# One-hot tiles of the first expert index made on ScalarE by Square and Relu, in 4 of the first 16 batches and in all from the 17th on

## What is computed

```python
q = (hb @ w_q).reshape(C, PEER_HEADS, 2, PEER_DK_HALF)
s = jnp.einsum('thpd,hpnd->thpn', q, sub_keys).astype(jnp.float32)
sv, si = lax.top_k(s, PEER_TOPK)
cand = sv[:, :, 0, :, None] + sv[:, :, 1, None, :]
cidx = si[:, :, 0, :, None] * PEER_NKEYS + si[:, :, 1, None, :]
...
fv, fpos = lax.top_k(cand, PEER_TOPK)
eidx = jnp.take_along_axis(cidx, fpos, axis=-1).reshape(C, PEER_HEADS * PEER_TOPK)
g = jax.nn.softmax(fv, axis=-1).reshape(C, PEER_HEADS * PEER_TOPK)
a = jax.nn.gelu(jnp.einsum('ted,td->te', u_tab[eidx], hb), approximate=False)
return jnp.einsum('te,ted->td', (g * a).astype(hb.dtype), v_tab[eidx])
```

## Time and profile before

| | |
|---|---|
| median of 3 runs | 2018.72 us (2017.43 to 2019.43) |
| the profiled execution | 2019.02 us, span 2017.2 us |
| TensorE matmuls | 1965.7 us busy, 97% |
| VectorE | 1407.0 us, 70% |
| ScalarE | 478.5 us, 24% |
| GpSimd | 919.2 us, 46% |
| DMA | 527.06 MB, 261 GB/s over the span |

### The profile page before, as it was taken

How to read it: one execution, slowest core, us unless ns; L and a number is a source line. 1 busy time by engine, 2 the same in 40 slices (tenths; PEclk the granted TensorE clock), 3 DMA queues, 4 the chain that set the end, 5 groups by cost and what they waited for, 6 DMA issues and landing times.

```text
span 2017.2 us, 27236 instructions
## 1 busy us (share of the span) xinstructions
PE 1965.7 (97%) x10016; PEld 1446.1 (72%) x10016; DVE 1407.0 (70%) x3048; ACT 478.5 (24%) x1005; POOL 919.2 (46%) x683
## 2 busy tenths in 40 slices
PE   9999999999999999999999999999999999999997
PEld 7888875888868875788886666666666666666563
DVE  3742025333374567649999999999999999987767
ACT  4122233133563326621230010100101010010100
POOL 5444432427443753424424555554545544443333
PEclk9999999999999999999999999999999999999999
DMA  6555652515202411134379999999999999999998
GB/s 237 189 189 180 148 144 94 187 64 178 86 9 58 125 35 53 43 125 134 129 285 348 422 422 422 421 422 422 415 422 414 416 419 417 407 421 421 419 422 288
DMA packets 92914, 527.06 MB, mean 261 GB/s; under 512 B 10080, under 2 KB 14608, under 8 KB 43280
## 3 DMA queue, kind: packets, MB, share of 16 engines
q0 software_dynamic: 37728, 270.55, 33.1%
q1 hardware_dynamic: 49680, 246.95, 33.0%
q10 hardware_dynamic: 5408, 8.34, 2.0%
HBM read 518.46 MB, written 7.34 MB: 261 GB/s over the span
## 4 chain that ended last, share of the span: by engine, by line
DMA 28%; DVE 20%; PE 15%; POOL 5%; issue 3%; ACT 1%; DVEq 0%; POOLq 0%; ACTq 0%
DMA work<-in_peer_uv,consts 16%; DMA ring<-in_peer_uv,consts 12%; PE ps L854 9%; DVE tables L2144 3%; POOL work L2790 3%; DVE work L2119 2%; POOL ring L2790 2%; DVE ring L2119 2%; DVE hT L2144 1%; DVE ring L2101 1%; PE ps L1138 1%; PE ps L883 1%; DVE tmp L2178 1%; DVE work L1902 1%; DVE work L1895 1%
## 5 line engine op out<-in xcount | busy, mean ns | idle before, releaser
L1271 PE MATMUL ps<-work,tmp 128*128 128x512 f32 x1008 | 447.5, 597 | 21.0 <-DVE tmp L2178 20.9
L1246 PE MATMUL ps<-hT,work 128*128 128x256 f32 x1984 | 450.2, 381 | 0.0
L2697 POOL TENSOR_TENSOR w_lo<-ring,w_hi 128x1024 fp32r<-128x1024 f32 (+2 forms) x116 | 275.0, 2377 | 334.9 <-ACT w_hi L2249 334.9
L1246 PEld LDWEIGHTS ps<-hT,work 128*128 128x128 f32 x1984 | 373.0, 190 | 75.2 <-issue 29.7
L1271 PEld LDWEIGHTS ps<-work,tmp 128*128 128x128 f32 x1008 | 189.3, 190 | 246.0 <-issue 213.9
L2790 POOL DMA_INDIRECT ring<-in_peer_uv,consts x128 | 237.7, 1857 | 264.8 <-DVE tables L2144 234.9
L2790 POOL DMA_INDIRECT work<-in_peer_uv,consts x128 | 226.3, 1768 | 258.1 <-DVE tables L2144 210.3
L2249 ACT ACTIVATE w_hi<-ring 128x1024 fp32r<-128x1024 f32 (+2 forms) x116 | 120.4, 1041 | 360.1 <-PE ps L854 335.3
L2119 DVE CUSTOM_DVE_ANT_0 ring<-ring,tables 128x1024 f32<-128x1024 f32 x128 | 155.5, 1221 | 52.3 <-DMA ring<-in_peer_uv,consts 50.1
L854 PE MATMUL ps<-w_hi,x_hi 128*128 128x512 f32 (+2 forms) x480 | 184.1, 384 | 1.1 <-DVE tmp L1667 1.1
L2119 DVE CUSTOM_DVE_ANT_0 work<-work,tables 128x1024 f32<-128x1024 f32 x128 | 155.2, 1221 | 42.5 <-DMA work<-in_peer_uv,consts 41.8
(11 more groups left out here) (380 smaller groups left out, 3108.8 us busy)
## 6 DMA issues: line engine op xcount, KB each, us to landing
work<-in_peer_v SPq DMA_DIRECT2D x64, 1024.0 KB
work<-in_u_steps SPq DMA_DIRECT2D x62, 1024.0 KB
ring<-in_a_w_in SPq DMA_DIRECT2D x48, 512.0 KB, 4.1
ring<-in_ada_w SPq DMA_DIRECT2D x48, 512.0 KB, 4.9
ring<-in_peer_w_q SPq DMA_DIRECT2D x32, 512.0 KB, 3.5
ring<-in_a_w_out SPq DMA_DIRECT2D x16, 512.0 KB, 4.1
ring<-in_b_w_in SPq DMA_DIRECT2D x16, 512.0 KB, 4.3
ring<-in_c_in SPq DMA_DIRECT2D x12, 512.0 KB, 3.7
```

Of the source, the lines that this page charges most:

```text
L1246: mm = pe.matmul(ps[:, 4 + s, j * DT:(j + 1) * DT], u[:, s, j, k, :], hT[:, k, GATHERED * P:T], start=(k == 0), stop=(k == KD - 1))
L1271: mm = pe.matmul(ps[:, 2 * t + half, :], tmp[:, s, j * DT + t * P:j * DT + (t + 1) * P], v_ring[:, s, j, half * BANK:(half + 1) * BANK], s ...
L2697: pool.tensor_tensor(w_lo[q % NPIECE][:, 0:n], ring[:, at:at + n], w_hi[q % NPIECE][:, 0:n], ALU.subtract).then_inc(w_split, 1)
```

## The change

ScalarE makes the one-hot of the first index for batches 3, 5, 7 and 11 of region 0 (`ACT_HOT`) and for all batches from 17 on. For each of the 16 tokens it computes (i - x)^2 over the 128 values x, the token's index i being the bias, a column of a new f32 copy of the indices (`i_cols`), and then over the whole tile Relu(1 - square), which is 1 where x is i and 0 elsewhere. In region 0 these four tiles have buffers of their own, in the expert buffers 1, 2 and 5, and the work is cut in halves: half of a tile a turn of the loop, eight squares ahead of the loop. The gathers into those buffers get waits for the spreads that read them: slot 1 for spread 5, slot 2 for spread 7, slot 5 for spread 11. In the steps ScalarE makes batch n+17 in step n, ahead of its copy of the gates of batch n+16.

The late pieces of head 0 stand after batches 0 to 3 instead of 1 to 4. `LATE_AT` is new: four products go ahead of the first spread, one product only follows spreads 4, 6 and 10, and the last late scores follow spread 3 instead of spread 5.

```diff
-LATE_AT = (0, 4, 10, 16, 22, 28, 32, 35, 38, 41, 44, 47, 50, 53, 56, 56, 56)
+LATE_AT = (4, 10, 18, 24, 30, 31, 34, 35, 38, 41, 44, 45, 48, 51, 54, 56, 56)
+LAST_SCORES = 3
+ACT_HOT = (3, 5, 7, 11)
...
+        i_cols = consts[:, NKEYS + 2 * GATHERED * SLOTS:NKEYS + 2 * GATHERED * SLOTS + DT]
+        act_hot = [twins(v) for v in (experts[1][:, 0:D], experts[1][:, D:2 * D], experts[2][:, 0:D], experts[5][:, 0:D])]
...
# TensorE
+            late_products(0, LATE_AT[0])
+            for m in range(RSTEPS):
+                if m in ACT_HOT:
+                    pe.wait_ge(hot_act, ACT_HOT.index(m) + 1)
+                    spread_gates(m, m % 2, act_hot[ACT_HOT.index(m)])
+                else:
+                    spread_gates(m, m % 2, hot_i[m % 2])
+                if m == LAST_SCORES:
+                    key_scores("pqL", "peer_l", 2 * PEER_H - 1, 2 * PEER_H - 1)
+                late_products(LATE_AT[m], LATE_AT[m + 1])
...
-                            spread_gates(n + RSTEPS, s)
+                            pe.wait_ge(hot_act, n + 4)
+                            spread_gates(n + RSTEPS, s, hot_i[s])
...
# VectorE
                 one_hot_j(0, m)
-                one_hot_i(m)
+                if m not in ACT_HOT:
+                    one_hot_i(m)
                 weighted_j(m)
-                if 1 <= m <= 4:
-                    late_piece(0, 3 + m)
+                if m < 4:
+                    late_piece(0, 4 + m)
...
-                    one_hot_i(n + RSTEPS)
+                    if n == 0:
+                        one_hot_i(n + RSTEPS)
...
# ScalarE
+            def square_i(m, buf, tokens=range(BATCH)):
+
+                for t in tokens:
+                    token = m % RSTEPS * BATCH + t
+                    act.activation(buf[:, t // TWIN, :, t % TWIN], iota[:], ACT.Square, scale=-1.0,
+                                   bias=i_cols[:, token:token + 1]).then_inc(squared, 1)
+                squares[0] += len(tokens)
+
+            def hot_from_squares(buf):
+
+                act.wait_ge(squared, squares[0])
+                act.activation(buf, buf, ACT.Relu, scale=-1.0, bias=astat[:, 0, 0:1]).then_inc(hot_act, 1)
+
             act.sem_inc(spread_kept, 2)
+            for i in range(3):
+                drained(act, "pairs", i)
+            act.wait_ge(one_made, 1)
+            act.activation(i_cols, iT, ACT.Copy).then_inc(i_kept, 1)
+            act.wait_ge(i_kept, 1)
+            first, second = range(0, BATCH // 2), range(BATCH // 2, BATCH)
+            square_i(ACT_HOT[0], act_hot[0], first)
             for m in range(RSTEPS):
...
+                hot, half = divmod(m + 1, 2)
+                if hot < len(ACT_HOT):
+                    if hot == 3 and half == 0:
+                        full(act, "pqL", 2 * PEER_H - 1)
+                    square_i(ACT_HOT[hot], act_hot[hot], (first, second)[half])
+                    if half:
+                        hot_from_squares(act_hot[hot])
...
             for n in range(STEPS):
                 if 1 <= n < STEPS - RSTEPS:
                     gelu(n + 1)
+                if n + 1 + RSTEPS < STEPS:
+                    act.wait_ge(spread_summed, n + 1 + RSTEPS + 1)
+                    square_i(n + 1 + RSTEPS, hot_i[(n + 1) % 2])
+                    hot_from_squares(hot_i[(n + 1) % 2])
                 if n + RSTEPS < STEPS:
                     act.wait_ge(dense_coef, n + 1)
                     keep_gates(n // RSTEPS + 1, n + RSTEPS)
...
# GpSimd
+            pool.memset(astat[:, 0, 0:1], 1.0).then_inc(one_made, 1)
...
+                    for last_hot, at in ((1, 1), (2, 2), (3, 5)):
+                        if slot == at:
+                            pool.wait_ge(spread_summed, ACT_HOT[last_hot] + 3)
```

More of the change, by code:

```diff
@@ L647, in network @@
         spread_summed = sem("spread_summed")
+        one_made = sem("one_made")
+        i_kept = sem("i_kept")
+        squared = sem("squared")
+        hot_act = sem("hot_act")
         last_sum = sem("last_sum")
@@ L1229, in _, with spread_gates @@
             key_scores("pqL", "peer_l", LATE_FIRST - 1, LATE_FIRST - 1)
-            def spread_gates(m, s):
+            def spread_gates(m, s, hot):
                 pe.wait_ge(hot_ready, m + 1)
@@ L1236, in spread_gates @@
                     for part in range(PARTS):
-                        mm = pe.matmul(ps[:, 6 + s, t * RKEYS:(t + 1) * RKEYS], hot_i[s][:, t // TWIN, :, t % TWIN],
+                        mm = pe.matmul(ps[:, 6 + s, t * RKEYS:(t + 1) * RKEYS], hot[:, t // TWIN, :, t % TWIN],
                                        hot_j[s][part][:, t // TWIN, :, t % TWIN], start=(part == 0), stop=(part == PARTS - 1))
@@ L1279, in _, with late_products @@
                 pe.wait_ge(bank_free[b], jobs.uses[b])
[L1280 to L1285, removed]
+            def late_products(at, end):
+                while at < end:
                     unit, k = divmod(at, KD)
-                    ks = ALL[k:min(KD, k + LATE_AT[m + 1] - at)]
+                    ks = ALL[k:min(KD, k + end - at)]
                     at += len(ks)
@@ L1301, in _ @@
                 dense_u(n, 16, range(0, 1))
-                spread_gates(n + RSTEPS, n)
+                if n:
+                    pe.wait_ge(hot_act, n + 4)
+                spread_gates(n + RSTEPS, n, hot_i[n])
                 dense_u(n, 16, range(1, PAIR))
@@ L2597, in late_exps @@
                                    accum_out=e_sum[:, h, u:u + 1]).then_inc(late_exp, 1)
-            act.sem_inc(spread_kept, 2)
+            squares = [0]
+            def square_i(m, buf, tokens=range(BATCH)):
[7 more added lines that the diff above has]
+                act.activation(buf, buf, ACT.Relu, scale=-1.0, bias=astat[:, 0, 0:1]).then_inc(hot_act, 1)
+            act.sem_inc(spread_kept, 2)
+            for i in range(3):
[5 more added lines that the diff above has]
+            square_i(ACT_HOT[0], act_hot[0], first)
             for m in range(RSTEPS):
@@ L2607, in _ @@
                         keep_late(LATE_FIRST + unit)
-                if LATE_AT[m] == KD * LATE_LEFT + 4:
+                if m == LAST_SCORES:
                     keep_late(2 * PEER_H - 1)
```

## The result

The change makes the kernel slower by less than one measurement of it can tell: 2022.04 us (22 runs) against 2019.33 us (22 runs) beside it, ratio **1.0014 (1.0008 to 1.0020)**, +2.7 us with bounds of 1.6 and 4.0. A second comparison, five rounds more, gave 1.0012 (1.0003 to 1.0021). The profiled execution took 2024.3 us, span 2022.1 us; ScalarE is busy for 817.0 us (40%) in place of 478.5, VectorE for 1353.6 (67%) in place of 1407.0.

A forecast was written before the change was run, and what follows sets the result against it. The prediction took the loop as bound by bytes, with VectorE full while transfer time is lost before it. It summed 5.0 (late stage) + 1.5 (clock) - 1.0 (regained) = +5.5 us, giving 2024.2 us, range 2014.5 to 2028.

The forecast's parts named there:

- What bounds the kernel now: Whole kernel: the long loop is bound by bytes; only transfer time lost before the queues fill, 13.9 and 9.8 us, matters.
- What ScalarE has to do for it: Region 0: 6.7 us of ScalarE a batch delays copies of gates; spread 9 +5.3 us, VectorE's end +5.0 us.
- What VectorE saves: Region 0: four one-hots less save VectorE 4.5 us; at best the stage ends 3.1 us sooner.
- The clock: TensorE in region 0: one drop to the lower clock level behind spread 9, +1.5 us.
- Transfers: GpSimd's gathers around region 0: new waits issue slots later, but VectorE gets them in time; price 0.
- What comes back: First steps: VectorE, 1.04 us lighter a step, frees gathers sooner; 0.3 to 2.8 us regained, taken as -1.0.
- smaller losses after 1088: Steps behind the hole at 1080 to 1084: 1.7 us of lost transfer time, counted in the bound of what is regained.
- The rule on table loads: ScalarE's loop turn: if Square were outside Gelu's set, two loads, 2.6 us, make it 10.8 of 14.9 us, still hidden.
- Late, but absorbed: Rival: stage +3.5 us, no clock drop, 2 us regained by the lighter VectorE; 2020.2 us, chance 0.18.
- my own case: The main forecast: region 0 ends late through ScalarE, +5.5 us in sum, 2024.2 us; own range 2021 to 2028, chance 0.57.
- ScalarE keeps up: Rival: squares start 0.20 us apart or less, region 0 ends 3.1 us sooner; 2014.8 us, chance 0.20.
- ScalarE bounds the loop: Rival: squares double in cost, 13 us a loop turn, region 0 15 us later; 2035 us or more, chance 0.05.

The follow-up runs named there:

- wide squares: The change, but in region 0 the squares of eight tokens are one instruction over 128x1024 with the first token's index as bias; 0.9980 of the kernel before.
- the three batches: The change with region 0's batches 3, 6 and 11 on ScalarE, squares in small pieces, late products moved; 0.9980 of the kernel before, 0.9988 without the steps' part.
- region 0 alone: The change with the one-hots of batches 17 to 63 left on VectorE; 1.0016 of the kernel before, repeat 1.0018.
- gather waits alone: The kernel before with only GpSimd's three new waits (slot 1 for spread 5, 2 for 7, 5 for 11); 0.9999 of the kernel before.

## Why the prediction was right, and where it was off

The forecast was +5.5 us, of which +2.7 (1.6 to 4.0) came: sign and mechanism right, size double. The 2022.04 us lie inside the range, but that is 13.5 us wide. And +2.7 us is 0.14%, within the 0.2% to which the prediction gave 0.22, not in the "slower" to which it gave 0.58.

- **"What bounds the kernel now"**: right. Every kernel's time agrees, within its interval, with the transfer time that it lost before the queues filled, and the loop's rate did not move.
- **"What ScalarE has to do for it"**: right, the moments even to a tenth. Squares stand 0.29 us apart (16 in 4.81 us), each lasting 0.43 in place of 0.38; the rectifier takes 2.00. Less the 1.63 us of the late start, copy 5 begins at 1040.50 (forecast 1040.5), spread 7 at 1041.22 (1041.2), copy 7 ends at 1048.78 (1048.8), spread 9 stands at 1048.92 (1048.9) and the first dot product at 1060.67; +5.2 for a forecast of +5.0. The tenth is in part luck: ahead of copy 5, ScalarE's waits for TensorE's queries came to 1.2 us (0.70 and 0.51) in place of 1.9, and the batches, queries and scores took about as much more than forecast. The wide squares show the cause.
- **"What VectorE saves"**, -3.1 us at best: near. The wide squares and the three batches take 1.4 and 1.5 us off the stage and have 1.3 and 1.2 us of waits for ScalarE left in it, which makes 2.7 without them, if those waits count in full (an estimate; no run is without them).
- **"The clock"**, +1.5: **wrong, it cost nothing new.** The drop came one spread sooner than I put it, behind the 3.41 us wait of spread 7, and its 1.1 us (2.66 - 1.54) ended inside TensorE's next wait for ScalarE, which would have been longer by as much. Three profiles show the trade: these six products take 2.91, 2.66 and 2.55 us (region 0 alone, after, region 0 alone again), the wait before spread 9 is 1.78, 2.01 and 2.13 us, and the stage is 47.97, 47.97 and 47.98. Behind the 2.01 us before spread 9, where I priced it, no row is slow. I added as a cost of its own what lies in the shadow of another wait. The drop at step 0, 8.80 us for 16 products, was there before too (8.54).
- **"Transfers"**, 0: borne out as far as it was tested, by the gather waits alone and by the wide squares, which gain with all three waits in place. Slots 5 and 7 went out at 1053.65 and 1061.15 by the old start; forecast 1053, and 1061 to 1062.
- **"What comes back"**, -1.0: **mis-sized, it was -1.9** alone and -1.6 behind the late stage. The first window, with the hole at 1080 to 1084, gave 0.5 us, near the 0.3 that I had worked out; what I left in the bound were the "smaller losses after 1088", and 1.1 us went in the window from 1096 on. My reason for the low end was that TensorE's loads come in unchanged. That it did not hold is shown by the windows; that the transfers missing there were gathers, which wait for VectorE, is argued only. In the loop the price is 0, as forecast.
- **The rule on table loads** did not come into play: 816 squares stand beside Gelu and Exp, and the number of table loads is 20 before and after. So squares and rectifier are 6.8 us of ScalarE's turn (4.81 + 2.00), and no load comes on top.

With the terms put right the sum is 5.2 + 0 - 1.9 = +3.3 us (+3.6 with the 1.6 measured behind the late stage), and 0.37 us outside the span, on which the prediction has no word, comes on top: 3.7 to 4.0 us, at the upper end of the measured interval. *Late, but absorbed* (2020.2) names what happened to a third of the delay better than my own case does, by another size: not +3.5 and -2, but +5.2 and -1.9. *ScalarE keeps up* is what the wide squares made true, and *ScalarE bounds the loop* fell, since the loop's rate stayed.

What stays open: a laying of the three batches without the last wait of 1.2 us, and four batches with the last rectifier ahead of the table load, were not tried. Nor were three batches in the coarse halves of the change, so how much of the gain of the three is their number and how much their placing is open.

## What to carry to other kernels

Work moved to an idle engine is paid where that engine's queue is in order: look not at its share of busy time but at who waits for what stands behind the new work, and play that queue through instruction by instruction. Moved work that comes as many small instructions can cost as much in their fixed part as in their elements, here 1.34 of 2.48 us; put it in pieces that fit between two deliveries, and where a batch must be made whole, take fewer. Do not add delays of one engine that fall into another's shadow, and do not judge a change of two parts by its total: here one part alone gained and the other, as laid out, lost more.

## What the runs showed of the hardware

The lower clock level (1.2 in place of 2.4 GHz) is not a fixed companion of a wait. TensorE waits 1.5 to 2.0 us for L2197 (or its twin) at the head of step 0 in all 13 profiles, and its next 16 products took 8.54 to 8.80 us in eleven of them and 7.11 in two, one of these a kernel whose repeat took 8.80. So one profile's clock can shift a sum by 1.4 to 1.7 us (8.54 or 8.80, less 7.11): compare such sums by more than one profile.

A square over 128 elements takes 0.43 us, over 1024 elements 1.14: an estimated 0.33 us is a fixed part by these two, and eight small ones cost 2.48 us where one wide one costs 1.14. The Trainium skill (ScalarE: Activation LUTs, What ACT_TABLE_LOAD costs) gives some 280 ns plus 0.833 ns an element with a pointer for the bias; that is an estimated 0.39 and 1.13 us, and the trace agrees on the wide one and is 0.04 us above on the small one.
